# Standing weights against both halves of the tokens' values in one 512-column matmul

## The reference, cut to what matters

```python
h = silu(x @ w_gate) * (x @ w_up);  x = x + h @ w_down        # feed-forward, 2 layers
q, k, v, g = split(x @ ret_w_in)                              # retention, 2 layers
a, g = split(x @ cf_w_pw1);  h = (a + b1) * sigmoid(g + b2)   # conformer
b, c, u = split(x @ sc_w_in);  y = (b * conv(c * u)) @ sc_w_out
h = relu(x @ mlp_w1) ** 2;  x = x + norm(h @ mlp_w2)          # MLP, 4 layers
```

## Time and profile before

| | before |
|---|---|
| median of 3 runs (lowest to highest) | 2044.52 us (2042.51 to 2044.65) |
| the profiled execution: its time, its span | 2043.73 us, 2041.9 us |
| granted TensorE clock, mean | 0.997 |
| busy: TensorE, VectorE, ScalarE, GpSimd | 2016.1, 1261.7, 938.1, 53.2 us |
| matmuls | 12782 |
| moved by DMA | 351.37 MB, 172 GB/s |

### The profile page before, as it was taken

How to read it: one execution, slowest core, us unless ns; L and a number is a source line. 1 busy time by engine, 2 the same in 40 slices (tenths; PEclk the granted TensorE clock), 3 DMA queues, 4 the chain that set the end, 5 groups by cost and what they waited for, 6 DMA issues and landing times.

```text
span 2041.9 us, 29543 instructions
## 1 busy us (share of the span) xinstructions
PE 2016.1 (99%) x12782; PEld 1774.8 (87%) x12782; DVE 1261.7 (62%) x1339; ACT 938.1 (46%) x1064; POOL 53.2 (3%) x89
## 2 busy tenths in 40 slices
PE   8999999999999999999999999999999999999998
PEld 6789998888999898789889689989899889778997
DVE  5766555686555665675557775556755566667554
ACT  6554443654543533444445554444544453335443
POOL 0000000000000000010000000000000000000000
PEclk9999999999999999999999999999999999999999
DMA  7324655442555565445555545546465555455553
GB/s 251 110 97 135 213 169 166 135 145 97 200 186 188 173 197 169 162 164 196 176 195 188 163 157 195 186 165 214 168 211 186 186 183 180 155 169 172 194 186 103
DMA packets 186179, 351.37 MB, mean 172 GB/s; under 512 B 15937, under 2 KB 27585, under 8 KB 186050
## 3 DMA queue, kind: packets, MB, share of 16 engines
q1 hardware_dynamic: 185474, 348.75, 51.4%
q10 hardware_dynamic: 576, 0.73, 0.1%
HBM read 344.31 MB, written 1.05 MB: 169 GB/s over the span
## 4 chain that ended last, share of the span: by engine, by line
PE 93%; DMA 2%; DVE 2%; ACT 2%; issue 1%; ACTq 0%; SPq 0%; DVEq 0%
PE psD L2049 15%; PE psD L2050 15%; PE psD L2054 13%; PE psD L2033 11%; PE psD L2034 11%; PE psD L2038 11%; PE psD L2052 2%; ACT wh L655 1%; PE psD L2362 1%; DVE wl L1135 1%; DMA raw<-in_w_in 1%; PE psD L2316 1%; DMA raw<-in_w_down 1%; PE psD L2435 1%; PE psD L2436 1%; PE psD L2036 1%
## 5 line engine op out<-in xcount | busy, mean ns | idle before, releaser
L1135 DVE TENSOR_TENSOR wl<-raw,wh 128x2048 fp32r<-128x2048 f32 (+2 forms) x327 | 723.3, 2219 | 442.5 <-ACT wh L655 440.0
L655 ACT ACTIVATE wh<-raw 128x2048 fp32r<-128x2048 f32 (+2 forms) x327 | 604.8, 1855 | 535.0 <-PE psD L2052 244.5
L2033 PE MATMUL psD<-AHL,wh 128*128 128x256 f32 x2112 | 599.2, 284 | 0.1
L2034 PE MATMUL psD<-AHL,wh 128*128 128x256 f32 x2112 | 597.4, 283 | 0.0
L2038 PE MATMUL psD<-AHL,wl 128*128 128x256 f32 x1976 | 558.9, 283 | 0.0
L2033 PEld LDWEIGHTS psD<-AHL,wh 128*128 128x128 f32 x2112 | 404.8, 192 | 2.7 <-issue 0.7
L2034 PEld LDWEIGHTS psD<-AHL,wh 128*128 128x128 f32 x2112 | 405.0, 192 | 1.9
L2038 PEld LDWEIGHTS psD<-AHL,wl 128*128 128x128 f32 x1976 | 378.8, 192 | 0.0
L2049 PE MATMUL psD<-wh,HH 128*128 128x512 f32 x880 | 351.3, 399 | 1.8 <-DVE wl L1135 1.8
L2050 PE MATMUL psD<-wl,HH 128*128 128x512 f32 x880 | 348.5, 396 | 0.0
L2054 PE MATMUL psD<-wh,HL 128*128 128x512 f32 x748 | 295.9, 396 | 0.0
(11 more groups left out here) (373 smaller groups left out, 1831.5 us busy)
## 6 DMA issues: line engine op xcount, KB each, us to landing
raw<-in_mlp_w SPq DMA_DIRECT2D x128, 1024.0 KB, 5.2
raw<-in_ret_w_in SPq DMA_DIRECT2D x48, 1024.0 KB, 5.1
raw<-in_w_gate SPq DMA_DIRECT2D x20, 1024.0 KB, 5.2
raw<-in_w_up SPq DMA_DIRECT2D x20, 1024.0 KB, 5.1
raw<-in_w_down SPq DMA_DIRECT2D x20, 1024.0 KB, 5.3
raw<-in_ret_w_out SPq DMA_DIRECT2D x16, 1024.0 KB, 5.1
raw<-in_w_in SPq DMA_DIRECT2D x15, 1024.0 KB, 5.3
raw<-in_cf_w_pw SPq DMA_DIRECT2D x12, 1024.0 KB, 5.3
```

The source lines that it names most:

```text
L655: e.activation(wh[q % NHL][:, 0:kt * n], raw[q % NRAW][:, 0:kt * n], ACT.Copy).then_inc(*up("act_wh", q))
L1135: e.tensor_tensor(wl[q % NHL][:, 0:kt * n], raw[q % NRAW][:, 0:kt * n], wh[q % NHL][:, 0:kt * n].bitcast(F32), ALU.subtract).then_inc(*up( ...
L2033: e.matmul(o, hi[:, k, fs], xh, start=kk == 0 and f % 2 == 0, stop=False, skip_group_check=True)
L2034: e.matmul(o, hi[:, k, fs], xl, start=False, stop=False, skip_group_check=True)
```

## The change

52 of the 66 units with standing weights are made in another way: b = 2 to 5 of gate and up in both feed-forward blocks, column blocks 1, 2, 3 of both retentions, the last two units of the conformer, the last four of the short convolution, and b = 2 to 7 of the four MLPs. In these units

- a chunk is 8 row blocks by 256 columns instead of 4 by 512 (`halves` in `weight_chunks`), of the same size;
- `cols_half` makes two feature tiles from one chunk. The high weights meet AH and AL in one matmul whose 512 columns are the 256 tokens of AH and the 256 of AL. It fills one bank: high x high in columns 0 to 255, high x low in 256 to 511. The low weights meet AH in a matmul of 256 columns that adds into the second half of the bank;
- a unit takes both pairs of banks, one for each half;
- ScalarE copies the first halves of the two banks into SBUF (`first_part`), then VectorE adds the second halves to the copy (`second_part`). What came after, and read PSUM, now reads this sum;
- the steps between (`high_to`, `low_to`, the waits) are put anew around the halves. `RPAIR` gives the pairs of the retention's eight units.

The diff, cut to its core (the retention, the conformer and the short convolution are changed like the feed-forward block and the MLP):

```diff
+    def halves(w, col):
+        for h in range(2):
+            chunks.append((w[:, col + 256 * h:col + 256 * (h + 1)].rearrange("(k p) n -> p k n", p=P), 8, 256))
...
             if b < NM:
-                matrix(A["mlp_w1"][i], b * 512, 512, DM)
+                if b < 2:
+                    matrix(A["mlp_w1"][i], b * 512, 512, DM)
+                else:
+                    halves(A["mlp_w1"][i], b * 512)
...
+            def first_part(o, pair, c):
+                e.wait_ge(*at("pe_used", c))
+                return e.activation(o, psD[pair][:, :, 0:S], ACT.Copy)
...
+            def second_part(o, pair):
+                return e.tensor_tensor(o, psD[pair][:, :, S:2 * S], o, ALU.add)
...
+            def cols_half(c, pair):
+                hi, lo = tiles(wh, c), tiles(wl, c)
+                both = AHL[:, :, :].rearrange("p (a k) n -> p k a n", a=2)
+                e.wait_ge(*at("dve_wl", c))
+                for k in range(8):
+                    for f in range(2):
+                        o = psD[pair][:, f, :]
+                        fs = slice(f * P, (f + 1) * P)
+                        e.matmul(o, hi[:, k, fs], both[:, k, :, :], start=k == 0, stop=False, skip_group_check=True)
+                        if k == 7 and f == 1:
+                            e.matmul(o[:, S:2 * S], lo[:, k, fs], AH[:, k, :], start=False, stop=True, skip_group_check=True).then_inc(*up("pe_used", c))
+                        else:
+                            e.matmul(o[:, S:2 * S], lo[:, k, fs], AH[:, k, :], start=False, stop=k == 7, skip_group_check=True)
...
 # mlp on TensorE
-                            unit(c, 2 + b % 2)
+                            for h in range(2):
+                                if b > 2:
+                                    e.wait_ge(*at("dve_mlp", "ra", i, b - 1, h))
+                                elif h:
+                                    e.wait_ge(*at("act_mlp", "relu", i, 1))
+                                else:
+                                    e.wait_ge(*at("dve_mlp", "lo", i, 0))
+                                cols_half(c + h, 2 + h)
 # mlp on ScalarE, b from 2 on
-                        high_to(c + 3)
-                            e.activation(r4, four(2 + b % 2), ACT.Relu)
+                        high_to(c + 2)
+                                e.wait_ge(*at("dve_mlp", "lo", i, b - 2))
+                                for h in range(2):
+                                    first_part(r4[:, 2 * h:2 * h + 2, :], 2 + h, c + h)
+                                    if h == 0:
+                                        high_to(c + 3)
 # mlp on VectorE, b from 2 on
-                            e.tensor_tensor(r4, r4, r4, ALU.mult)
+                                for h in range(2):
+                                    rh = r4[:, 2 * h:2 * h + 2, :]
+                                    low_to(c + 2 + h)
+                                    e.wait_ge(*at("act_mlp", "part", i, b, h))
+                                    second_part(rh, 2 + h)
+                                    e.wait_ge(*at("dve_mlp", "ra", i, b, h))
+                                    e.scalar_tensor_tensor(rh, rh, 0.0, rh, ALU.max, ALU.mult)
 # ffn on TensorE, b from 2 on
-                            e.wait_ge(*at("dve_ffn", "rg", l, b - 1))
-                            unit(c, 2)
-                            e.wait_ge(*at("dve_ffn", "h", l, b - 1))
-                            unit(c + 2, 3)
+                            for h in range(2):
+                                if b == 2:
+                                    e.wait_ge(*at("dve_ffn", "h" if h else "rg", l, 1))
+                                else:
+                                    e.wait_ge(*at("dve_ffn", "ua", l, b - 1, h))
+                                cols_half(c + h, 2 + h)
+                            for h in range(2):
+                                e.wait_ge(*at("dve_ffn", "ga", l, b, h))
+                                cols_half(c + 2 + h, 2 + h)
```

More of the change, by code:

```diff
@@ L218, in weight_chunks @@
         elif kind == 1:
-            for col in (1024, 0, 1536, 512):
+            for col in (1024, 0):
                 matrix(A["cf_w_pw1"][0], col, 512, DM)
+            for col in (1536, 512):
+                halves(A["cf_w_pw1"][0], col)
             first["y", i] = len(chunks)
@@ L224, in weight_chunks @@
         else:
-            for col in (1024, 2048, 0, 1536, 2560, 512):
+            for col in (1024, 2048):
                 matrix(A["sc_w_in"][0], col, 512, DM)
+            for col in (0, 1536, 2560, 512):
+                halves(A["sc_w_in"][0], col)
             first["y", i] = len(chunks)
@@ L1034, in conformer @@
+                for h in range(2):
+                    first_part(HP[:, 4 + 2 * h:6 + 2 * h, 30:S + 30], 2 + h, c + 2 + h).then_inc(*up("act_cf", "ap", h))
+                    high_to(c + 5 + h)
+                c += 4
                 e.wait_ge(*at("dve_cf", "hp", 5))
                 e.wait_ge(*at("pool_set", "hp"))
+                e.wait_ge(*at("pe_used", c - 1))
                 four_taps(e, "b", (2, 3), "dma_xb1")
@@ L1073, in gated_high, with halves @@
                         e.activation(HH[j // 2][:, 2 * (j % 2):2 * (j % 2) + 2, :], VT[:, 2 * j:2 * j + 2, :], ACT.Copy).then_inc(*up("act_sc", "ah", j))
+                def halves(c, o, name, free):
+                    high_to(c + 2)
+                    if free is not None:
+                        e.wait_ge(*at("dve_sc", *(free if isinstance(free, tuple) else ("gated", free))))
+                    for h in range(2):
+                        first_part(o[:, 2 * h:2 * h + 2, :], 2 + h, c + h).then_inc(*up("act_sc", "part", name, h))
+                        if h == 0:
+                            high_to(c + 3)
                 for b in range(2):
-                    high_to(c + 3)
+                    if b:
+                        halves(c, VT[:, 4:8, :], "c", None)
+                    else:
+                        high_to(c + 3)
                     c += 2
@@ L2602, in retention @@
                     elif nb == 0:
-                        cols_chunk(c, 2 + n % 2, 0)
+                        cols_chunk(c, RPAIR[n], 0)
                         spread_scale(2 * i + 4)
-                        cols_chunk(c + 1, 2 + n % 2, 4)
+                        cols_chunk(c + 1, RPAIR[n], 4)
                     elif nb < 4:
-                        unit(c, 2 + n % 2)
+                        for h in range(2):
+                            if nb > 1:
+                                e.wait_ge(*at("dve_ret", i, "qa", nb - 1, h))
+                            elif h:
+                                e.wait_ge(*at("dve_ret", i, "si", 0))
+                            cols_half(c + h, 3 - h)
                     else:
-                        rows_unit(c, 2 + n % 2, act_tile)
+                        rows_unit(c, RPAIR[n], act_tile)
                     c += 2
@@ L2669, in conformer @@
                         e.wait_ge(*at("act_cf", "sig", 0, 3))
-                        unit(c, 2)
-                        e.wait_ge(*at("dve_cf", "ag", 0))
-                        unit(c + 2, 3)
+                        cols_half(c, 2)
+                        e.wait_ge(*at("dve_cf", "ag", 0, 0))
+                        cols_half(c + 1, 3)
+                        for h in range(2):
+                            e.wait_ge(*at("dve_cf", "ga", h))
+                            cols_half(c + 2 + h, 2 + h)
                     c += 4
```

281 lines of the change are left out of this document (185 added, 96 removed).

## The result

| | before | after |
|---|---|---|
| median of 5 runs (lowest to highest) | 2044.52 us (2042.51 to 2044.65) | 2033.57 us (2033.47 to 2038.65) |
| profiled execution: time, span | 2043.73, 2041.9 us | 2038.56, 2036.5 us |
| granted TensorE clock, mean | 0.997 | 0.995 |

The ratio of after to before is 0.9961, with a 95% interval of 0.9947 to 0.9975: the change makes the kernel some 5 to 11 us faster. That lies inside the range of the prediction (2012 to 2040), but it is about half of the gain forecast (20 us, 2024.5) or less: the medians differ by 11 us, and by the ratio the gain is 8 us. The five runs of after fall in two groups, three at 2033.5 us with a mean clock of 0.997 and two at 2038.6 with 0.995.

The account below looks back on a forecast made before the run. The prediction took TensorE's own time per matmul as the bound. From 2043.73 us it took 21.5 for removed starts, added 1.5 for new waits and 0.8 to reach the median: 2024.5 us, range 2012 to 2040.

Parts of the forecast that it names:

- What bounds the kernel: Whole kernel: TensorE, busy 2016.1 of 2041.9 us, has almost no idle time; only its own time per matmul can shorten it.
- How many starts go: In the 52 changed units: one matmul start per weight tile goes, 1664 in all, with the multiplied columns unchanged at 768.
- What one start is worth: Changed weight tiles: 346.5 ns instead of 359.4, 12.9 less on each of 1664, a gain of 21.5 us.
- a sign of being wrong: Changed tiles: the prediction is wrong if the pair of starts takes over 355 ns or under 340.
- the dear 512: Rival, changed units: the new 512-column matmul is spaced like the hidden rows' 233.3 ns, giving 2035.5 us; chance 0.14.
- More than the start: Rival, changed units: the 256-column matmul also gets shorter, its weights in place early; 2008 us, halfway 2016; chance 0.11.
- No gain: Rival, changed units: the moving operand's two pieces cost two starts, giving 2046 us, no change; chance 0.03.
- A cheap start: Rival, changed units: the merged matmul keeps most of the 12.9 ns; 2.6 ns a tile goes, 2041.7 us; chance 0.03.
- The waits: TensorE's new waits for half-unit drains in retention, conformer gate and short convolution: 1.5 us together, between 0 and 6.
- slower: Rival, units outside the MLPs: ScalarE's weight copy precedes the drain, TensorE waits 1.2 us a half; 2091 us; chance 0.07.
- The cover of the new copies and additions: Half-unit drains: 62 us more on ScalarE and 71 on VectorE, spread over engines idle for 1100 and 780 us.
- 1 MB in rows of 1 KB: Weight transfers of 104 chunks: each lands in 6.2 us, between 5.2 and 7.6, hidden and costed at 0.

Follow-up runs that it names:

- long runs: The changed kernel with all sixteen 512-column matmuls of a half unit first, then the sixteen of 256 columns: 2027.73 us, ratio 0.9926 to before.
- a push at the entry: The changed kernel with one more matmul of 128 columns at the start of each half unit, its result overwritten: one run, 2046.84 us.
- the first run: The changed kernel with the high and low activations of a row block side by side in AHL: 2036.69 us, ratio 0.9959 to before.

## Where the prediction failed and where it held

**What bounds the kernel.** Right: TensorE keeps 99% of the span, and its time per matmul is what moved.

**How many starts go.** Right: 1664 fewer matmuls.

**What one start is worth.** This is the step that failed: "A changed tile then takes 226.7 + 119.8 = 346.5". Each price was right for its own form (227.1 alone; 226.9 and 119.4 in long runs). The step took them as prices of an instruction, whoever its neighbours are. Alternating, the 512 measured 235.6 and the 256 116.6. A pair settles in one of two patterns, 346.7 or about 353, and 1664 tiles came to 352.3 on average: 7.4 ns saved on each instead of 12.9, 12.3 us instead of 21.5. An MLP unit got 0.21 us shorter instead of 0.4. The cheaper pattern is the price of the sum, so the step missed by the 88 of 104 half units that fell into the dearer one. Three runs rest this on the sequence and the entry: the same matmuls grouped by two (348.4 over all tiles), by sixteen (347.6), and with a push at the entry (353.6 and 346.6 in neighbouring halves). The pieces of the operand, the half of the bank and the place of `HH` and `HL` were each tried and left the average within 0.7 ns. The shift by 12 bytes didn't: it turned most units to the cheaper pattern, 348.2 on average, with the sequence as it was. So a good part of what the step missed was settled by chance of the layout, and nobody aimed at it.

The prediction named a sign of being wrong, a pair over 355 or under 340. 352.3 lies between the two, with 43% of the step's gain gone: the sign was set too wide to catch it. The total came inside the stated range because the range also held the case of the dear 512.

**The rivals.** In size the case was "the dear 512" (353.1 a tile, 2035.5 us, a chance of 0.14). Its reason, that the new matmul is spaced like those of the hidden rows, is wrong: moving `HH` and `HL` takes the hidden rows from 233 to 227 and leaves the tiles at 353. "More than the start" had one part right, the 256 got shorter (116.6 where 119.8 was taken), but the 512 got dearer by more. "No gain" by the two pieces fell with the first run. "A cheap start" had 2.6 ns a tile where 7.4 came.

The rule in the Trainium skill's "TensorE: Matmul & The Clock Gate", section "Back-to-back issue gap", one column per clock plus about 2.5 ns from start to start, is given there for matmuls without the weight loads of a stream. Worked out from it, an estimate for the new tile is 325.0. The trace, in which every matmul has a weight load, disagrees: the lowest unit of after has 346.7 a tile.

**The waits.** The sum had 1.5 us and the trace shows about 2.5, but at other places. The drains of the retention, the feed-forward blocks and the short convolution, with a margin of 0.7 us, are in no wait of TensorE that the trace lists; VectorE's 8.84 of 11 us in the retention (8.05 before) stayed below one. The rival "slower" named the mechanism that did come up at one place: a weight copy ahead of a drain. Its argument against it, that "the order written out puts that copy behind the drain", holds for the drain of the same half but not for the next one: in the conformer the copy behind the first drain is ahead of the second. (It is so in the MLPs too, but there its weights have landed and it is over in time.) And the price wasn't the copy's 1.92 us but the wait for its transfer, 6.44 us, as SyncE had issued the taps ahead of it. At 1 half of 104 it cost about 1.3 us.

**The rest.** The cover of the new copies and additions held (VectorE 77.7 us more, 71 expected for the additions; ScalarE 30.5, as the ReLU copies went). 1 MB in rows of 1 KB lands in 5.5 us (6.2 taken, 5.2 to 7.6 allowed), and is hidden. Of the clock the prediction said nothing. The profiled execution has 4.7 us in the mixers that go with it, and the median run little.

## What to carry to other kernels

The distance between two starts is a price of the sequence and its entry, not of an instruction: where forms are to be mixed, read it from a stretch that mixes them in the same way, or keep forms in runs and lay the sum on that. When the same instruction shows two prices at two places (227 and 233), change where its operands lie before taking either. When a drain is cut in two, look at what stands in the queue between the halves, and at what that can be waiting for.

## What was not expected of the hardware

- Alternating 512 and 256 columns, each behind a new weight tile, settle in a pattern of 346.7 or about 353 ns a pair and keep it for a half unit at least. The same instructions give both, in one execution. What chooses at the entry stays open: no run set it at will. The distance from the last hidden-row start to the first of the changed stretch went with it in after (231 to 234 ns dearer, 240 cheaper).
- A standing tile read from `HH` and `HL` at their old place cost 233.2 ns a matmul of 512 columns, some 36 KB nearer to the start of the partition 227, 13.8 us over the kernel. Twelve bytes made no difference to them. Whether it is how far in they lie, or what lies around them, wasn't tried.
- With two long and two short in turn, the short ones cost 114.5 and 116.1, less than the 119.4 among their like, and the long ones more (233.0 and 233.2 against 226.9). Their sum is 348.3 a tile against 347.1.
- The granted clock fell to the lower level for 6.8 us at 427 us in the profiled execution of after, and not in that of before, in a stretch of unchanged code. Two of the five runs of after show the lower mean (0.995).
